# Moving the second tile's value projection ahead of the first gate projection, and loading the third head's query weights into the slot it leaves

## The reference, cut to what matters

```
proj = x @ w_in, split into q, k, v, iq, ik, iw, z, xbc, dt
attention (8 heads x 64): an indexer scores all causal keys, the best 64 per query are kept; softmax; p @ v
SSD      (8 heads x 64): conv and SiLU on xbc, chunked scan (chunk 128), y * silu(z), RMS norm
mix = concat(attention, SSD) @ w_out
h   = LayerNorm(alpha * x + mix)
q   = h @ wq                                  (8 heads x 2 sides x 128)
per head: 16 best of 128 keys on each side -> the 16 best pairs -> 16 experts and their softmax gates
out = LayerNorm(alpha * h + sum over 8 x 16 experts of gelu(h . u[e]) * gate * v[e])
```

## Time and profile before

| | |
|---|---|
| median of 3 runs | 805.42 us (805.28 to 806.05) |
| the profiled execution's own time | 807.17 us |
| its span, first to last instruction | 805.4 us |
| PE busy | 549.3 us (68%) |
| DVE busy | 548.6 us (68%) |
| ACT busy | 450.2 us (56%) |
| POOL busy | 283.9 us (35%) |
| moved by DMA | 301.08 MB, 268.45 MB of it in the 256 gathers |
| share of the chain that ended last | DMA 45%, DVE 20%, PE 19%, issue 8%, ACT 5%, POOL 3% |

### The profile page before, as it was taken

How to read it: one execution, slowest core, us unless ns; L and a number is a source line. 1 busy time by engine, 2 the same in 40 slices (tenths; PEclk the granted TensorE clock), 3 DMA queues, 4 the chain that set the end, 5 groups by cost and what they waited for, 6 DMA issues and landing times.

```text
span 805.4 us, 10125 instructions
## 1 busy us (share of the span) xinstructions
PE 549.3 (68%) x3340; PEld 455.4 (57%) x3340; DVE 548.6 (68%) x1395; ACT 450.2 (56%) x805; POOL 283.9 (35%) x267
## 2 busy tenths in 40 slices
PE   7999999998957878565545454609554645454695
PEld 4486497776857778454445454608454644454642
DVE  3488487898654767676757576399767767676554
ACT  1125138778744666666565566529665656566532
POOL 0000004536613345444434444307644444444400
PEclk9999999999978989867878787758777668777689
DMA  7992017999999999999999999999999999999992
GB/s 258 390 392 90 0 54 239 422 421 421 422 418 421 420 421 420 421 421 422 419 422 420 422 421 422 421 422 360 421 421 422 423 422 421 422 423 422 422 422 111
DMA packets 51433, 301.08 MB, mean 374 GB/s; under 512 B 5696, under 2 KB 8000, under 8 KB 17600
## 3 DMA queue, kind: packets, MB, share of 16 engines
q0 software_dynamic: 36864, 268.45, 80.6%
q1 hardware_dynamic: 12144, 30.67, 10.2%
q10 hardware_dynamic: 2384, 1.44, 0.6%
HBM read 299.49 MB, written 1.05 MB: 373 GB/s over the span
## 4 chain that ended last, share of the span: by engine, by line
DMA 45%; DVE 20%; PE 19%; issue 8%; ACT 5%; POOL 3%; DVEq 0%; SPq 0%; another core or an unknown queue 0%; POOLq 0%; ACTq 0%
DMA arena<-in_expert_uv,expert 43%; PE bank L488 5%; DVE arena L1548 4%; PE bank L679 4%; PE bank L659 3%; POOL arena L459 3%; ACT arena L1009 2%; PE bank L500 2%; PE bank L603 2%; DMA ln_gb<-in_w_in 2%; ACT weight L999 1%; PE bank L622 1%; DVE score L1527 1%; DVE picked L1528 1%; DVE big L1258 1%
## 5 line engine op out<-in xcount | busy, mean ns | idle before, releaser
L659 PE MATMUL bank<-ident,arena 128*128 128x128 f32 x1920 | 299.2, 325 | 237.1 <-ACT arena L1009 235.7
L459 POOL DMA_INDIRECT arena<-in_expert_uv,expert x256 | 282.2, 1102 | 479.2 <-PE bank L659 261.9
L1548 DVE SCALAR_TENSOR_TENSOR arena<-x_sb,arena 128x1024 f32<-128x1024 f32 x256 | 307.0, 1224 | 172.6 <-DMA arena<-in_expert_uv,expert 165.1
L659 PEld LDWEIGHTS bank<-ident,arena 128*128 128x128 f32 x1920 | 275.1, 171 | 263.1 <-ACT arena L1009 258.6
L1009 ACT ACTIVATE arena<-arena,weight 128x1024 f32<-128x1024 f32 x240 | 257.5, 1141 | 2.2
L994 ACT ACTIVATE gelu<-dots 128x4 f32<-128x4 f32 (+2 forms) x76 | 15.6, 205 | 223.6 <-DVE arena L1548 214.4
L999 ACT ACTIVATE weight<-gelu,gate 128x1 f32<-128x1 f32 x256 | 56.1, 286 | 3.5
L488 PE MATMUL bank<-arena,x_t 128*128 128x512 f32 (+1 forms) x128 | 53.8, 576 | 4.8 <-DMA x_t<-in_x_columns 4.8
L488 PEld LDWEIGHTS bank<-arena,x_t 128*128 128x128 f32 x128 | 25.3, 203 | 27.0 <-issue 25.3
L622 PE MATMUL bank<-x_t,arena 128*128 128x128 f32 x256 | 29.9, 275 | 0.0
L679 PE MATMUL bank<-arena,mid 128*128 128x512 f32 x64 | 29.4, 622 | 0.0
(11 more groups left out here) (227 smaller groups left out, 488.9 us busy)
## 6 DMA issues: line engine op xcount, KB each, us to landing
arena<-in_w_in SPq DMA_DIRECT2D x5, 2048.0 KB, 17.5
arena<-in_w_out SPq DMA_DIRECT2D x2, 2048.0 KB, 19.3
arena<-in_expert_uv,expert POOLq DMA_INDIRECT x256, 28.1
arena<-in_peer_wq SPq DMA_DIRECT2D x4, 1024.0 KB, 9.4
mix<-in_peer_wq SPq DMA_DIRECT2D x2, 1024.0 KB, 5.2
big<-in_peer_wq SPq DMA_DIRECT2D x2, 1024.0 KB, 4.9
arena<-in_w_idx ACTq DMA_DIRECT2D x4, 304.0 KB, 5.7
x_t<-in_x_columns SPq DMA_DIRECT2D x4, 256.0 KB, 5.2
```

The costliest lines, as they stand in the source:

```text
L459: pool.indirect_dma_start(out=arena[:, slot * SLOT:(slot + 1) * SLOT], out_offset=None, in_=expert_uv, in_offset=bass.IndirectOffsetOnAxis ...
L659: last = mm(banks[2 * tile + k // 4][:, (k % 4) * P:(k % 4 + 1) * P], lhsT=arena[:, at + k * P:at + (k + 1) * P], rhs=ident[:, :], is_tran ...
L1548: ins = stt(rows, x_rows[:, bass.ds(tile * D_MODEL, D_MODEL)], 1.0, rows, ALU.mult, ALU.mult, accum_out=dots[:, parity, j:j + 1])
```

## The change

Three things are done in code, and the list of slots is rewritten to match.

1. `project(("proj_v", 1), ...)` is taken out of the expert part and runs as one piece directly behind `project(("proj_v", 0), ...)`, in front of the first gate projection `proj_z` of tile 0. ACT's `take_v(1)` moves with it.
2. The eight transposes of tile 1's q and k, and ACT's two copies of them, move in front of both, since the values of tile 1 overwrite the q that they read.
3. SP's code is the same, but its wait for `("proj_v", 1)` now ends before the load of head 1 is issued, so head 2's load follows that of head 1 at once.
4. `first_slots()` puts slot 5 first. The reuse distance stays: from the 16th gather on, the n-th gather waits for the same use count as before.

```
-    jobs += [...] + probs[0] + [("proj_v", 0), ("proj_z", 0), ("cb", 0), ("T_xs", 0), ("pv", 0)]
+    jobs += [...] + probs[0] + [("T_qk", 0, 1), ("T_qk", 1, 1), ("proj_v", 0), ("proj_v", 1), ("proj_z", 0), ...]
...
-    start = [10, 11, 12, 13, 14, 15, 1, 10, 11, 12, 13, 5, 14, 15, 0, 1]
-    grow = [10, 11, 12, 13, 5, 14, 15, 0, 1, 10, 11, 2, 12, 8, 9, 13]
-    ring = [6, 7, 5, 14, 15, 0, 1, 10, 11, 2, 12, 8, 9, 13]
+    start = [5, 10, 11, 12, 13, 14, 15, 1, 5, 10, 11, 12, 13, 0, 14, 15]
+    grow = [1, 5, 10, 11, 12, 13, 0, 14, 15, 1, 5, 2, 10, 8, 9, 11]
+    ring = [6, 7, 12, 13, 0, 14, 15, 1, 5, 2, 10, 8, 9, 11]
...
             pe.wait_ge(w_in_sem["v"], 16)
-            project(("proj_v", 0), "v", 0)
+            transposed_qk(0, 1)
+            transposed_qk(1, 1)
+            for t in range(TILES):
+                project(("proj_v", t), "v", t)
             pe.wait_ge(w_in_sem["z"], 16)
...
-            transposed_qk(0, 1)
-            transposed_qk(1, 1)
             transposes(("T_b",), [xbc[:, 4 + g, 0:P] for g in range(GROUPS)])
...
             scores_of_keys(0, 1)
-            project(("proj_v", 1), "v", 1, ks=range(0, 4))
             sum_group(0, 1)
-            project(("proj_v", 1), "v", 1, ks=range(4, KT))
             sum_group(0, 2)
...
             silu_xbc(0, 1)
+            take_qk(0, 1)
+            take_qk(1, 1)
             take_v(0)
+            take_v(1)
             take_mixed("T_attn", 0, attn_t_ready, 0)
...
-            take_v(1)
```

More of the change, by code:

```diff
@@ L61, in psum_jobs @@
     jobs += [("proj_k", 0)] + idx_dots[0] + [("proj_k", 1), ("T_qk", 0, 0), ("T_qk", 1, 0)] + idx_dots[1] + sums[0] + logits[0]
-    jobs += [("proj_xbc", 0, 0), ("proj_xbc", 0, 1)] + probs[0] + [("proj_v", 0), ("proj_z", 0), ("cb", 0), ("T_xs", 0), ("pv", 0)]
+    jobs += [("proj_xbc", 0, 0), ("proj_xbc", 0, 1)] + probs[0] + [("T_qk", 0, 1), ("T_qk", 1, 1), ("proj_v", 0), ("proj_v", 1), ("proj_z", 0), ("cb", 0), ("T_xs", 0), ("pv", 0)]
     jobs += [("T_attn", 0), ("y_diag", 0), ("out", 0, 0), ("T_y", 0), ("out", 0, 1)]
-    jobs += [("T_qk", 0, 1), ("T_qk", 1, 1), ("T_b",)] + sums[1] + logits[1][0:2] + [("T_h", 0, 0), ("T_h", 0, 1)] + logits[1][2:4]
+    jobs += [("T_b",)] + sums[1] + logits[1][0:2] + [("T_h", 0, 0), ("T_h", 0, 1)] + logits[1][2:4]
     jobs += [("first_q",), ("peer_q", 0, 0), ("first_scores",), ("state",), ("key_scores", 0, 0), ("proj_xbc", 1, 0), ("proj_xbc", 1, 1)] + probs[1] + [("proj_z", 1), ("peer_q", 0, 1)]
-    jobs += [("key_scores", 0, 1), ("proj_v", 1), ("pv", 1), ("cb", 1), ("T_xs", 1), ("y_off",), ("T_attn", 1), ("y_diag", 1), ("peer_q", 0, 2)]
+    jobs += [("key_scores", 0, 1), ("pv", 1), ("cb", 1), ("T_xs", 1), ("y_off",), ("T_attn", 1), ("y_diag", 1), ("peer_q", 0, 2)]
     jobs += [("key_scores", 0, 2), ("out", 1, 0), ("out", 1, 1), ("T_y", 1), ("peer_q", 0, 3), ("key_scores", 0, 3)]
@@ L1047, in _ @@
             take_mixed("T_y", 4, y_t_ready, 0)
-            take_qk(0, 1)
-            take_qk(1, 1)
             take_b()
```

## The result

The changed kernel takes 812.15 us (median of 4, 810.94 to 812.75); beside it on the same chip the kernel before takes 805.73 us (4 runs). The ratio is 1.0069, with an interval of 1.0055 to 1.0083: slower by 4.4 to 6.7 us, 5.6 in the middle. (The quotient of the two medians is 1.0080, or 6.4 us; the text goes by the recorded ratio, which has an interval.) The forecast had the sign. Its 809.9 us is 2 us short of the median, which lies outside the forecast's own range of 808.6 to 811.2 us and inside the range of 8 in 10; its +4.5 us is 1.1 short of the ratio, at the lower edge of the interval. In the profiled executions 807.17 us became 811.77 us (span 805.4 to 810.0), +4.6. One such pair can stand a us or two beside the medians.

The account below looks back on a forecast made before the run. PE bounds the kernel until the first gather, the DMA stream from 140 us. 7.5 - 2.49 - 2.49 + 2.1 = +4.6, rounded to +4.5 us: median 809.9 us, own range 808.6 to 811.2, 8 in 10 806.8 to 813.0.

Parts of the forecast that it names:

- Nothing hides the projection in front: On PE before the first gather: no idle time takes `proj_v(1)`, so all of it delays `h`, +6.9 us.
- The start, +7.5 us: First gather later by projection 6.9 plus transposes 0.87 less a vanished wait 0.26, at about 127.8 us.
- the wait that goes: PE's wait for ACT's SiLU before line 553 disappears because PE arrives later: -0.26 us.
- Two units of -2.49 us each: DMA stream: slot 5's extra early gather and head 2's earlier load each take one 1,048,576-byte unit out, -2.49 us each.
- The removed halves give back nothing: The 6.88 us of projection removed from PE behind the first gather counted as zero; other bound, all 6.88 given back.
- The gathers up to about the 25th are asked for 7.5 us later: DVE starts and ends its unbroken run 7.5 us later, so slots free and gathers are requested 7.5 us later.
- +2.1 us: Around the 22nd gather: the stock of 4.7 us shrinks by 5.0, runs dry by 0.3, and restarting costs 1.8.
- the prediction's own sign: A stream rate down for over 5 us after 150 us would mean rival B holds.
- rival B: Nothing given back: the queue empties more than once, late requests decide, +6 to +7.5 us, about 812.4 us; chance 0.10.
- The dip near 550 us: DMA rate dip belonging to tile 0's last LayerNorm: said to be untouched and to move along with the stream.
- Rival A: The stream never runs dry and one unit stays in hand: +2.5 us, 807.9 us; chance 0.20.
- Rivals C and D: C: projection's 6.9 us hidden, about 802 us, chance 0.05. D: removed piece repays the front, 805.4 us, chance 0.07.

Follow-up runs that it names:

- e7_only_delay: Kernel before with tile 1's q and k transposes moved forward and eight dummy matmuls in front of `proj_z(0)`, nothing removed behind: 813.93 us, ratio 1.0093.
- e1_head2_late: Changed kernel with head 2's load held back until head 1's key scores are done: 812.24 us, ratio 1.0063 to the kernel before.
- e3_filled_hole: Changed kernel with four dummy matmuls where each half of the value projection stood: 811.89 us, ratio 1.0066 to the kernel before.
- e11_delay_and_cut: The kernel of e7_only_delay with 7/8 of head 2's load left out (head 2's results wrong): 811.53 us, ratio 1.0063 to the kernel before.
- the candidate: Kernel before with `proj_v(1)` behind head 0's key scores, `proj_z(1)` in the two halves, head 1's queries earlier, lists adapted: 805.54 us, ratio 0.9995.
- e12_gate_late: Changed kernel with ACT's exponentials of the third head's gates moved behind the eighth group of scaled slots: 812.39 us, ratio 1.0063 to the kernel before.

## Why the prediction was right in sign and short in size

- **Nothing hides the projection in front: right.** `transposed_h(0)` is 6.9 us later, and `e7_only_delay`, which has the delay and nothing else, is 7.5 us slower, 6.8 in its span.
- **The start, +7.5 us: 0.6 too much.** 0.3 of it is that PE came to the projections 0.3 us sooner in this execution (65.17 against 65.46 us for the transposes ahead of them); the projections grew by 15.62 - 8.75 = 6.87 us and the transposes took 0.87, as predicted. Of the other 0.3, 0.2 is the wait that goes: from the first projection to line 553 it was 9.00 us and is 15.45, only 6.45 more, so it gave back 0.4 and not 0.26. The last 0.1 goes between line 553 and `transposed_h(0)`.
- **Two units of -2.49 us each: right up to 165 us.** There the stream is 1.9 us behind, which is 6.9 less 5.0.
- **The removed halves give back nothing: right, and a cost was missed.** They left PE a hole of 3.8 us and a clock of 0.50 behind it, and the requests come 7.8 us late instead of 7.5. Filling the hole took 0.9 us off these requests and nothing measurable off the kernel.
- **"The gathers up to about the 25th are asked for 7.5 us later": not the 14th.** The new list of slots puts slot 0, which waits for `attend(1)`, one place earlier, and the 14th gather is asked for 10.5 us later (9.6 with the hole filled, 6.9 in the delay-alone kernel, which has before's list). That is where the stream first runs thin. It isn't what the kernel pays for in the end: with head 2's load late, the stream is full from 165 to 170 us (421 GB/s) and the kernel is no faster.
- **"+2.1 us" for the stream that runs dry is the term that was mis-sized.** The window loses 3.85 us. The prediction let the stream run at full rate until its stock was gone, and then added a restart. It never ran dry: it ran for 25 us at 358 GB/s. By the prediction's own sign (a rate that is down for over 5 us after 150 us) that is rival B. The terms of the error can be told apart. The requests are 7.8 us late on a stream that would be 1.9 late, so 5.9 us were asked of the spare time where I had 5.0; and the spare was 5.9 - 3.85 = 2.0 us, where 5.0 - 2.1 = 2.9 was assumed. So 0.9 us lies on each side. The 22nd gather, on which the prediction counted the stock, is not the tightest. From request to landing it has 10.1 us in before and 7.8 in after; the 18th has 9.7 and 6.7, the 20th 8.8 and 6.2, the 24th 8.4 and 6.4.
- **No restart of an empty queue came at the 22nd gather, where the prediction put one.** In after there is one at the first gather and one at the sixth, which is asked for at 142.33 us. The DMA's windows of 1 us (the columns of the earlier trace rows) are:

```profile
128.00:129.00 1.00, 1.00 (x11) 1.00 (x11) 0.97 (x4) 0.66 (x2) 0.70 (x2) 1.00 0.02 8
129.00:130.00 1.00, 1.00 (x11) 1.00 (x11) 0.82 (x5) 1.00 (x5) 0.69 (x2) 1.00 0.91 197
...
144.00:145.00 1.00, 1.00 (x11) 1.00 (x10) 0.84 (x2) 0.87 (x3) 0.70 (x2) 1.00 0.08 16
145.00:146.00 1.00, 1.00 (x11) 1.00 (x10) 0.00 (x0) 0.98 (x2) 0.74 (x1) 1.00 0.80 139
```

By the packets, 1.8 us pass from the first gather's issue to its first byte (127.20 to 128.99 us) and 2.9 from the sixth's (142.33 to 145.21). From the first gather's last byte to the last increment of its semaphore it is 0.4 us (132.39 to 132.76). So the trace again differs from the split of the fixed 2 us that the Trainium skill, DMA: Bandwidth & Descriptors, gives in its section on the anatomy of one DMA: for these gathers most of the time that is not transfer lies in front of the first byte.

- **The dip near 550 us was said to be untouched; it is 1.6 us smaller in after.** It is also 373 GB/s in `e1_head2_late`, 390 in `e3_filled_hole`, 393 in `e11_delay_and_cut` and 359 in the candidate, which differ in nothing there. It is 380 in `e7_only_delay`, as in before. What sets its size I haven't found; it adds or takes 1 to 2 us in a single execution.
- **Rival A (never dry, +2.5)** was right that the DMA doesn't empty at the 22nd gather and wrong on the price. **Rival B (late requests decide, +6 to +7.5)** is nearer in the medians, though the queue never empties behind the sixth gather. The stream is 5.7 us late, the requests less 2 us of spare, which the rival left out. (That these agree is no proof: a landing is its request plus the time to landing, so the second figure follows from the first.) **Rivals C and D** fell with the earlier trace rows and with DVE's router at 149.36 us.

The kernels with the delay, as a sum. "Late at 165" is the gathers' packets up to 165 us against before's; "lost" is 14,730 KB less what the windows from 165 to 200 us moved, at 421 GB/s; the 24th request is against 186.38 us; "by landings" is the 100th gather.

| kernel | late at 165 | lost 165:200 | sum | by landings | 24th request late | request to landing, 24th | ratio |
|---|---|---|---|---|---|---|---|
| after | 1.9 | 3.85 | 5.7 | 5.9 | 7.8 | 6.4 | 1.0069 |
| head 2's load late | 4.3 | 1.5 | 5.8 | 6.6 | 7.9 | 6.8 | 1.0063 |
| hole filled | 1.7 | 3.75 | 5.4 | 5.8 | 6.9 | 7.0 | 1.0066 |
| delay alone | 5.6 | 0 | 5.6 | 6.6 | 6.9 | 8.1 | 1.0093 |
| delay and cut | 5.0 | 0 | 5.0 | 5.1 | 7.3 | 6.1 | 1.0063 |

In the two last rows less of head 2's load has passed by 165 us than in before, which the column of gathers doesn't show, so their sums are somewhat off; the landings don't have this fault. The first three stand at 5.8 to 6.6 us by landings, although the stream of the second was a unit later at 165 us. Of the two units, 5 us, that were saved, about one at most was gained: 2 us by the ratios, 0.7 by landings. That a second unit is worth next to nothing is shown by `e1_head2_late` against after. That late requests are the reason rests on this account and isn't shown. Filling the hole brought the requests 0.9 us forward and the stream 0.1, as the time to landing grew from 6.4 to 7.0 us, so that time is no fixed floor; a kernel in which the requests alone come earlier, with both units saved, was tried (`e12_gate_late`) and missed its aim, so the direct proof is open.

## What to carry to other kernels

The runs here fit a stream that ends at the later of two sums: its bytes from its start, and its last tight request plus the time from a request to its landing. It is a way to count, and the second sum was not tested by itself. Before counting bytes saved as time saved, take from the trace how late the tightest request may come (here 2 us at the 24th gather), and count no saving beyond it. Work that was put in front of this stream's first request cost its full length (`e7_only_delay`); what is taken away behind has to bring the requests forward too. And when a list of buffers is reordered, look for each entry at what its buffer waits for: here slot 0, one place earlier, made one request 2.7 us later (9.6 against 6.9).

## What I had not expected of the hardware

- The rate falls by degrees when few gathers are outstanding: 310 GB/s with at most two, 369 with at most three, 421 in the full stream, with 1 MiB each. The busy share hardly shows it: 0.98 at 369 GB/s and 0.97 at the 358 of after, against 1.01 at 420. The rate has to be read, not the share.
- PE's clock fell to 0.50 in one idle gap of 3.8 us and stayed there until 161 us (1.2 instead of 2.4 GHz), in the middle of a stretch that stood at 1.00 in before; with the gap filled it stayed at 1.00 there and was 0.66 in 195 to 200 us, for which I have no cause.
- The dip near 550 us moved by up to 2 us between kernels that are alike there, with no cause that I can name. Differences of 1 us between two profiled executions mean little here; the ratios over many runs are what can be used.
